# One core, two transformer blocks in float32: a Sqrt table moved, a last addition given to TensorE, one rope job later, and 65 weight loads asked for by GpSimd

## The reference

```python
# first block: adaLN, RWKV-7 head group + short conv + Fourier mixer, then a SwiGLU feed-forward
sh1, sc1, ga1, sh2, sc2, ga2 = split(silu(c) @ w_mod + b_mod)          # 6 x 2048, also for c_ctx
px = modulate(rms_norm(x, norm_mix), sh1, sc1) @ w_in                  # 2048 -> 5568 columns
pc = modulate(rms_norm(ctx, norm_mix), csh1, csc1) @ w_in
_, s_ctx = rwkv_mix(rwkv_streams(conv3(pc)), (s_zero, s_zero))         # 16 heads of 64, two directions
yx_rw, _ = rwkv_mix(rwkv_streams(conv3(px)), s_ctx)
x = x + ga1 * (concat([yx_rw, short_conv(px), fourier(px)]) @ w_out)
x = x + ga2 * ffn(modulate(rms_norm(x, norm_ffn), sh2, sc2), w_gate, w_up, w_down)
x = rms_norm(x, norm_final)
# second block: adaLN, HGRN2 head group (8 heads of 128, two directions) + windowed attention, SwiGLU
p_lat, p_ctx = (modulate(rms_norm(t, norm_mix_g), sh, sc) @ w_in_2 for t in (x, ctx_2))
hg = hgrn2_mixer(p_lat[:, :HG], p_ctx[:, :HG])
at = window_attention(p_lat[:, HG:], p_ctx[:, HG:])                    # q and k: rms norm, then rope
x = x + gt_m * (concat([hg, at]) @ w_out_2)
x = x + gt_f * swiglu(modulate(rms_norm(x, norm_ffn_g), sh_f, sc_f), w_gate_up_2, w_down_2)
```

## Time and profile before

| | us |
|---|---|
| median of 3 runs | 3718.28 (3715.53 to 3718.54) |
| the profiled execution, its own time | 3715.66 |
| span of its trace (first to last instruction) | 3713.9 |
| TensorE busy in the span | 3584.2 (97%) |
| VectorE, ScalarE, GpSimd busy | 2228.2, 543.8, 136.5 |
| recurrent stage, about 168 to 1051 us of the span | 883 |

### The profile page before, as it was taken

How to read it: one execution, slowest core, us unless ns; L and a number is a source line. 1 busy time by engine, 2 the same in 40 slices (tenths; PEclk the granted TensorE clock), 3 DMA queues, 4 the chain that set the end, 5 groups by cost and what they waited for, 6 DMA issues and landing times. The chain is left out here.

```text
span 3713.9 us, 66568 instructions
## 1 busy us (share of the span) xinstructions
PE 3584.2 (97%) x29203; PEld 3053.5 (82%) x29203; DVE 2228.2 (60%) x4290; ACT 543.8 (15%) x1043; POOL 136.5 (4%) x137
## 2 busy tenths in 40 slices
PE   7989999999998999999999999999999999999999
PEld 4466666667788999999998557767777999999999
DVE  3265555655347888989777445554653766555543
ACT  2222222222101000000001222322222000000000
POOL 0000000000000000000001000000001000000000
PEclk9999999999999999999999999999999999999999
DMA  9723333334467778776677354444323766654554
GB/s 328 244 76 90 90 90 100 98 90 110 119 209 250 252 248 268 235 245 221 205 230 230 102 171 159 145 150 153 120 73 131 227 202 207 213 175 145 166 171 131
DMA packets 680786, 637.93 MB, mean 172 GB/s; under 512 B 42141, under 2 KB 670642, under 8 KB 679346
## 3 DMA queue, kind: packets, MB, share of 16 engines
q1 hardware_dynamic: 573968, 563.15, 47.7%
q10 hardware_dynamic: 106530, 70.54, 6.6%
HBM read 627.36 MB, written 6.29 MB: 171 GB/s over the span
## 5 line engine op out<-in xcount | busy, mean ns | idle before, releaser
L1926 PE MATMUL bank<-extra,work 128*128 128x128 f32 x4224 | 478.9, 275 | 0.0
L1926 PEld LDWEIGHTS bank<-extra,work 128*128 128x128 f32 x4224 | 475.2, 192 | 0.0
L653 DVE SCALAR_TENSOR_TENSOR work<-weight_ring,silu_c,work 128x256 f32<-128x256 f32 x1050 | 434.2, 488 | 0.0
L1926 PE MATMUL bank<-work,weight_ring 128*128 128x128 f32 x2816 | 327.9, 278 | 7.8 <-ACT work L2030 7.5
L1926 PEld LDWEIGHTS bank<-work,weight_ring 128*128 128x128 f32 x2816 | 321.7, 194 | 9.1 <-issue 8.6
L2099 DVE TENSOR_TENSOR work<-weight_ring 128x2048 f32<-128x2048 f32 (+1 forms) x76 | 129.3, 1701 | 287.1 <-DMA weight_ring<-in_w_gate_up 154.1
L999 PE MATMUL bank<-work,x_channels 128*128 128x256 f32 (+1 forms) x736 | 243.1, 466 | 6.5 <-DMA x_channels<-in_w_in 4.1
L1969 PE MATMUL bank<-work,weight_ring 128*128 128x128 f32 x2112 | 247.4, 275 | 0.0
L1969 PEld LDWEIGHTS bank<-work,weight_ring 128*128 128x128 f32 x2112 | 241.1, 192 | 0.2 <-DMA weight_ring<-in_w_down 0.2
L2503 PE MATMUL bank<-work,weight_ring 128*128 128x512 f32 x448 | 205.6, 604 | 1.0 <-PEq L2278 1.0
L999 PEld LDWEIGHTS bank<-work,x_channels 128*128 128x128 f32 x736 | 131.5, 192 | 71.0 <-issue 50.3
(11 more groups left out here) (420 smaller groups left out, 5249.8 us busy)
## 6 DMA issues: line engine op xcount, KB each, us to landing
weight_ring<-in_w_mod SPq DMA_DIRECT2D x80, 2048.0 KB, 10.5
weight_ring<-in_w_gate_up SPq DMA_DIRECT2D x44, 2048.0 KB, 9.5
weight_ring<-in_w_in SPq DMA_DIRECT2D x26, 2048.0 KB, 10.6
weight_ring<-in_w_down SPq DMA_DIRECT2D x32, 1536.0 KB, 7.1
weight_ring<-in_w_gate SPq DMA_DIRECT2D x22, 2048.0 KB, 8.2
weight_ring<-in_w_up SPq DMA_DIRECT2D x22, 2048.0 KB, 12.0
weight_ring<-in_w_down SPq DMA_DIRECT2D x32, 1280.0 KB, 6.3
weight_ring<-in_w_out SPq DMA_DIRECT2D x16, 2048.0 KB, 8.7
```

The costliest lines, as they stand in the source:

```text
L653: ins = v_.scalar_tensor_tensor(a, w[:, k, :], c, a, ALU.mult, ALU.add)
L1926: last = mm(out[:, m * P:(m + 1) * P], left[p][:, k, m * P:(m + 1) * P], right[p][:, k, :], start=k == 0, stop=k == 7)
```

## The change

In the opening the table-bringing square root goes ahead of the loop, and the wait for the sums and the two roots go from s = 1 to s = 0. In `RowSquares` the last of GpSimd's additions goes; TensorE multiplies the total of 15 tiles and then the last squared tile with ones, both into one PSUM group. In `MIX2` the job ("rk", 0) goes behind ("nq", 1) and ("aq", 6). In the recurrent stage the 65 loads from n = 4 on are asked for by GpSimd, each as four DMAs of 256 KB (`LOAD_PARTS`), 260 in all, after GpSimd's own wait for the end of the dense job that frees the buffer; `load(marks[hp, "value"])` stands ahead of GpSimd's wait for the diagonal blocks of hp and `load(marks[hp, "end"])` behind its four mask products. Their arrival is counted on semaphores of their own (`later_in0` to `later_in3`).

```diff
--- before.py
+++ after.py
@@ -441,6 +441,7 @@
                         act.wait_ge(S["scaled"], 2 * k + 2 - v)
                         a_(hT[:, k, seg[v]], hT[:, k, seg[v]], ACT.Identity, bias=st.mod[0][:, v, k:k + 1]).then_inc(S["h_ready"], 1)
+            a_(st.eps[:, 2:3], st.eps[:, 0:1], ACT.Sqrt)
             for s in range(MOD_FIRST):
                 if s and s % 2 == 0:
                     act.wait_ge(S["mod_kept"], s)
@@ -450,8 +451,6 @@
                     act.wait_ge(S["mod_columns"], s - 1)
                 nc.scalar.copy(mod_row[s % 2], st.psum[6 + s % 2][:, 0:256]).then_inc(S["mod_row"], 1)
                 if s == 0:
-                    a_(st.eps[:, 2:3], st.eps[:, 0:1], ACT.Sqrt)
-                if s == 1:
                     act.wait_ge(S["sumsq"], 2)
                     for v in range(2):
                         a_(rstd[:, v, :], st.psum[v][:, 0:T], ACT.Sqrt, bias=st.eps[:, 0:1], scale=1.0 / DM).then_inc(S["root"], 1)
@@ -762,8 +761,10 @@
         self.nc.gpsimd.tensor_tensor(self.total, self.total, self.buf[:, m % 2, :], ALU.add).then_inc(self.s_summed, 1)
     def finish(self, pe):
-        pe.wait_ge(self.s_summed, KT - 1)
-        self.nc.tensor.matmul(self.st.psum[4][:, 0:T], self.st.c("ones"), self.total, start=True, stop=True).then_inc(self.s_total, 1)
+        pe.wait_ge(self.s_summed, KT - 2)
+        self.nc.tensor.matmul(self.st.psum[4][:, 0:T], self.st.c("ones"), self.total, start=True, stop=False)
+        pe.wait_ge(self.s_squared, KT)
+        self.nc.tensor.matmul(self.st.psum[4][:, 0:T], self.st.c("ones"), self.buf[:, (KT - 1) % 2, :], start=False, stop=True).then_inc(self.s_total, 1)
@@ -805,6 +806,7 @@
 MOD_GROUP = 2
 FILL = {"first": 3.0, "value": 7.0, "ahead": 6.0, "solve": 9.0, "gram": 2.5, "between": 3.0, "rows": 3.0, "chain": 1.5, "step": 0.95}
 WBUFS = 4
+LOAD_PARTS = 4
 DENSE, DENSE_ENDS = dense_jobs()
 LOADS = [w for job in DENSE for w in dense_loads(job)]
 LOADS_UPTO = [sum(len(dense_loads(job)) for job in DENSE[:j]) for j in range(len(DENSE) + 1)]
@@ -982,7 +984,10 @@
             def weights_in(n):
                 if n == 0:
                     pe.wait_ge(st.s_first, 16)
-                W(f"dense_in{n % WBUFS}", 16 * (n // WBUFS + (n % WBUFS > 0)))
+                if n >= WBUFS:
+                    W(f"later_in{n % WBUFS}", 16 * LOAD_PARTS * (n // WBUFS))
+                elif n:
+                    W(f"dense_in{n}", 16)
                 return wbuf[n % WBUFS]
             def dense():
@@ -1323,18 +1328,7 @@
             a_(st.wd[0:LORA], st.wd[0:LORA], ACT.Tanh).then_inc(S("lora_act"), 1)
             a_(st.gd, st.gd, ACT.Sigmoid).then_inc(S("lora_act"), 1)
-            n_load, n_out = 1, 0
-
-            def load(upto):
-                nonlocal n_load
-                while n_load < min(upto, len(LOADS)):
-                    name, k0, k, c0, cols = LOADS[n_load]
-                    if n_load == 1:
-                        act.wait_ge(st.s_kept, 16)
-                    act.dma_start(wbuf[n_load % WBUFS].rearrange("p (k c) -> p k c", k=k),
-                                  st.dram[name][k0 * P:(k0 + k) * P, c0:c0 + cols].rearrange("(t p) n -> p t n", p=P)
-                                  ).then_inc(S(f"dense_in{n_load % WBUFS}"), 16)
-                    n_load += 1 if n_load > 1 else 3
+            n_out = 0
             def dense_out(upto):
@@ -1344,7 +1338,6 @@
                     j = n_out
                     kind, i = DENSE[j]
                     W("dense_mm", j + 1)
-                    load(LOADS_UPTO[j + 1] + WBUFS)
                     b = bank[6 + j % 2]
                     if j in RAW:
                         x = RAW.index(j)
@@ -1378,7 +1371,10 @@
                         nc.scalar.copy(st.ycf[:, 4 + i, :], b[:, 0:T]).then_inc(S("dense_out"), 1)
                     n_out += 1
-            load(WBUFS)
+            act.wait_ge(st.s_kept, 16)
+            name, k0, k, c0, cols = LOADS[1]
+            act.dma_start(wbuf[1].rearrange("p (k c) -> p k c", k=k),
+                          st.dram[name][k0 * P:(k0 + k) * P, c0:c0 + cols].rearrange("(t p) n -> p t n", p=P)).then_inc(S("dense_in1"), 16)
             def key_squares(hp):
                 if hp:
@@ -1474,11 +1470,32 @@
             g_ = nc.gpsimd
             g_.memset(P0, 0.0).then_inc(S("zeroed"), 1)
             off = c("off_half").unsqueeze(1).broadcast_to([P, 4, P])
+            n_load, n_job = WBUFS, 0
+
+            def load(jobs):
+                nonlocal n_load, n_job
+                for j in range(n_job, jobs):
+                    upto = min(LOADS_UPTO[j + 1] + WBUFS, len(LOADS))
+                    if n_load < upto:
+                        W("dense_mm", j + 1)
+                    while n_load < upto:
+                        name, k0, k, c0, cols = LOADS[n_load]
+                        to = wbuf[n_load % WBUFS].rearrange("p (k c) -> p k c", k=k)
+                        src = st.dram[name][k0 * P:(k0 + k) * P, c0:c0 + cols].rearrange("(t p) n -> p t n", p=P)
+                        for q in range(LOAD_PARTS):
+                            part = slice(q * k // LOAD_PARTS, (q + 1) * k // LOAD_PARTS)
+                            pool.dma_start(to[:, part], src[:, part]).then_inc(S(f"later_in{n_load % WBUFS}"), 16)
+                        n_load += 1
+                n_job = max(n_job, jobs)
+
+            load(marks[-1, "end"])
             for hp in range(NP1):
+                load(marks[hp, "value"])
                 W("blocks_out", 128 * (hp + 1))
                 for g in range(4):
                     x = Lm[:, 4 * g:4 * g + 4, :]
                     g_.tensor_tensor(x, x, off, ALU.mult).then_inc(S("off_ready"), 1)
+                load(marks[hp, "end"])
         @block.vector
         def _(dve):
@@ -1778,7 +1795,7 @@
         @block.gpsimd
         def _(pool):
             nc.clear_and_free_semaphores(st.spent)
-            for m in range(1, KT):
+            for m in range(1, KT - 1):
                 rows.add(pool, m)
         @block.scalar
@@ -2395,7 +2412,7 @@
             _jobs.insert(2, ("hn", _g - 1))
     else:
         _jobs = [("ak", 0), ("ak", 1), ("aq", 0), ("hn", 2), ("aq", 1), ("nk", 0), ("aq", 2), ("nk", 1), ("aq", 3), ("nq", 0), ("aq", 4),
-                 ("aq", 5), ("rk", 0), ("nq", 1), ("aq", 6), ("aq", 7), ("rq", 0), ("nq", 2), ("av", 0), ("nq", 3), ("av", 1), ("rq", 1),
+                 ("aq", 5), ("nq", 1), ("aq", 6), ("rk", 0), ("aq", 7), ("rq", 0), ("nq", 2), ("av", 0), ("nq", 3), ("av", 1), ("rq", 1),
                  ("rq", 2), ("av", 2), ("rq", 3), ("hn", 3), ("av", 3)]
     MIX2.append(_jobs)
 MIX2_JOBS = [job for group in MIX2 for job in group]
```

## The result

The changed kernel takes 3755.58 us in the median (3754.13 to 3761.33), the kernel before 3718.28: ratio 1.0102, 95% interval 1.0089 to 1.0116. It is 37.3 us slower; the forecast was 12 us faster. The profiled execution took 3755.59 us, its span is 3753.8.

The account below looks back on a forecast made before the run. TensorE's own stream, not bandwidth, was taken as the bound. Opening 2.4, sums of squares 0.8, hgrn 6.5 and recurrent loads 2.2 gave 11.9 us off 3718.3, about 3706 us; range 3701 to 3738, the forecast's own 3702 to 3711.

Parts of the forecast that it names:

- What bounds the kernel: Recurrent stage: bound by TensorE's own stream, not bandwidth; TensorE busy 840.9 of 883 us, 42 us idle.
- Opening: Opening: roots start at about 37.85 us instead of 40.29 and the chain to TensorE's projection moves up, 2.4 us won.
- Sums of squares: Finishes of out1 and out2: TensorE product replaces GpSimd's last addition; out2 wins 0.8 us, out1 0.
- Hgrn: Hgrn: TensorE's 6.51 us wait before a rope job goes, as two jobs now stand ahead of it; 6.5 us won.
- The moment of asking: Recurrent stage: GpSimd asks for loads at once where ScalarE asked late; at most 4.5 us won, 2.2 after lateness.
- A quarter's price: Recurrent stage: each quarter of a load costs GpSimd 1.5 us for w_in, 1.0 for w_mod.
- my upper bound of 2.7: Quarter of a load on GpSimd: at most 2.7 us, if each 256 KB waits for the one before to land.
- GpSimd as a queue: Recurrent stage: dearer quarters make loads late at two tight places; 3726 us at 2.2 each, 3746 at 2.7; chance 0.29.
- a wait at L1197: Recurrent stage: TensorE waiting there for GpSimd's mask products, 5.1 us for four, would show the forecast wrong.
- VectorE keeping GpSimd from writing: First tight place: some six VectorE instructions each hold up a quarter, 2.6 us less won, 3708.6 us; chance 0.06.

Follow-up runs that it names:

- the run with the small changes alone: Kernel before plus only the opening, sums of squares and hgrn order changes, recurrent stage as before: 3704.9 us, ratio 0.9969.
- The run with SyncE: Opening, sums of squares and hgrn changes on the kernel before, with loads 56 and 57 asked for by SyncE instead of ScalarE: 3703.7 us.
- the runs with 1024, 1280 and 1920 bytes: Changed kernel with each head pair's mask products put ahead of GpSimd's loads, at three sizes of space for written descriptors: 3736.6, 3712.5 and 3714.5 us.
- More space by itself: Changed kernel with 1920 bytes instead of 1024 for GpSimd's written descriptors, nothing else: 3757.3 us, ratio 1.0114.
- the run with late masks: Opening, sums of squares and hgrn changes on the kernel before, no GpSimd DMA, mask products waiting for a later dense job: 3731.2 us.
- eight parts: Changed kernel with eight DMAs to a load instead of four, space 1024 bytes: 3738.2 us, ratio 1.0065.

## Why the prediction was wrong, step by step

**What bounds the kernel.** Right: TensorE's stream. But I read the stage's 42 us of idle time only as something to be won. It was also the measure of how little slack the chains beside TensorE have: a few us of delay on VectorE turn up on TensorE, and then once more as a lower clock.

**Opening, 2.4 us.** The gap shrank by 2.3 us. In the changed kernel this was lost again in head pair 0, where the first mask products were held up by quarters and then held VectorE for 5.11 us (11.2 against 8.8 us of wait at the first products with the inverted blocks).

**Sums of squares, 0.8 us.** out2 as forecast: from the square's end to the last product's end 0.75 us instead of 1.54. In out1 too: from the last square's end to the last product's end there are 2.56 us in the changed kernel and 2.57 before, and the two pairs of products took 2.07 us where I had put 2.1, both at a granted clock of 0.50. In the run with the small changes alone the same products ran at 1.00 and took 1.13 us, so 0.95 us were won there; that belongs to the clock of that moment and was in no term.

**Hgrn, 6.5 us.** The wait went and none came. With the other two, 9.7 us forecast and 11.2 measured.

**The moment of asking, 4.5 us.** This step failed, though nothing hung on it in the end. "GpSimd asks at once: at most 4.5 us won" priced the wait for the load and did not look at what stood behind it: ScalarE's copy of the bank, equally late. The run with SyncE shows 4.47 us in its place.

**A quarter's price.** The sum's term "I take 1.5 us for a quarter with 512 runs" measured 3.6 to 3.7 in most places, outside even my upper bound of 2.7; the 1.0 for a w_mod quarter measured about 1.7 (four from 254.55 to 261.37). The mechanism of that bound (each quarter waits for the one before to land) was right for w_in; the size was wrong because I took the landing from ScalarE's and SyncE's rows; here a quarter landed about 3.3 us after it was issued. What decides is the space, as the runs with 1024, 1280 and 1920 bytes show. How it is counted is my estimate, fitted to six patterns: a DMA of n runs takes about n/16 + 1 entries of 16 bytes in each of 16 queues, 33, 17 and 9 for 512, 256 and 128 runs. Space 1024 holds 64: one, three and seven in flight, as seen; 1280 holds 80: two of 33 and four of 17, as seen; 1920 holds 120: three of 33, as seen. A count of n/16 with one entry kept free gives the same six, and no run parts the two. The Trainium skill, page "DMA: Bandwidth & Descriptors", section "Terms", has the 16-byte descriptors and their rings in SBUF, and the six patterns fit that size; that the rings' size sets the pace is what the runs add. So the rival "GpSimd as a queue" came true with a higher price. Its share, read from the runs with the masks first: 3736.6 - 3714.5 = 22 us.

**The mask products.** The prediction counted them as 5.1 us that stand in front of a load, and named a wait at L1197 for them; no such wait for GpSimd came. It never asked what stands in front of *them*, and what VectorE does when they come late. This is the step that failed by being left out, at no cost in the sum, with 3755.6 - 3736.6 = 19 us in this kernel and 26 us without any DMA, at another late place. I had the contention as a rival, in the other direction: VectorE keeping GpSimd from writing, 2.6 us. The changed kernel's trace shows GpSimd's DMA instructions at 0.70 to 0.89 us throughout, and VectorE standing still for its products. The Trainium skill, page "SBUF — State Buffer", section "Who interferes with whom", says that a VectorE instruction with two SBUF inputs, or in a two-port mode, cannot run beside a GpSimd instruction that reads SBUF, and that who issues first decides. On which instructions are held the traces agree: L1570 (two inputs) took 4.58 us instead of 0.75, the tensor_scalar L1568 4.85 instead of 0.43 (its mode no row shows), while the reciprocal L1569 overlapped the products by up to 1.8 us with its 3.35 us unchanged, and so did the products out of PSUM at 0.41 us which they meet in the kernel before. On who issues first they do not show it: a held instruction of the block inverse in head pair 0 stands in the trace 0.15 us ahead of the products (214.92 against 215.07). What the mask products met in the old place, VectorE's work out of PSUM, was the cover of that place, and I did not see that the change took it away.

**The whole.** 19 + 22 + 9.6 = 50.7 us for GpSimd's loads against 11.2 for the rest (37 to 40 us net). The split holds for this order of mending only: more space by itself won nothing (3757.3 against 3755.6), and with the masks first on top of it 43 us were won. The slower rival reached to 3746 and I cut the range at 3738.

## What to carry to other kernels

When work is added in front of an instruction on an engine with room to spare, follow that instruction, not the engine's busy share: where will it now run, and what runs there on an engine that it can hold still. GpSimd's queue of DMAs has a length; compare the runs of a DMA with the space reserved before counting on several in flight, and cut by runs, not by bytes. Before a wait is priced as a gain, move its end away in mind and name the next semaphore of the same instruction; here it was 4.5 us behind a 4.1 us wait.

## What the runs showed of the hardware that I had not expected

- A wait of 3.39 us in a stage that is otherwise full was followed by two lines of products that took 6.42 and 4.94 us; a head pair earlier in the same run, with no wait ahead of them, they took 3.75 and 2.82. The lower clock behind the wait cost 4.8 us, more than the wait.
- VectorE against four GpSimd products in a row: in the changed kernel one instruction stood still until all four had ended (3.7 to 5.1 us, seven times), while in the kernel before and in the run with late masks VectorE got instructions in between the products (0.8 to 1.7 us each). The traces of all runs with full mask products divide without exception: a VectorE instruction that met them was held until the fourth had ended in 20 cases, in all of which the products came within 0.11 us behind a DMA instruction of GpSimd (changed kernel, 1920 bytes, eight parts, masks first with 1024), and was let in between in 12 cases, in all of which GpSimd had been idle for over 4 us before them. Whether the DMA or the missing idle time is the cause was not tried.
- The tight places do not close with more space: some 5 us of wait for a load were left at each of the two with 1920 bytes, and up to 5.8 with 1280. Why was not followed up.
